# A two-layer backbone in one core: a new order of loads, parts and sums, and token low parts made on GpSimd

## The reference

```python
mod = jnp.split(silu_c @ w_ada[layer] + b_ada[layer], 6)      # mod_c for the context, likewise
a = modulate(rms_norm(h, g[0]), mod[0], mod[1])
o = mixer(a)                                                  # even_mixer or odd_mixer
h = h + mod[2] * rms_norm(o, g[1])
f = jnp.square(jax.nn.relu(modulate(rms_norm(h, g[2]), mod[3], mod[4]) @ w_ff1)) @ w_ff2
h = h + mod[5] * rms_norm(f, g[3])
```

## Time and profile before

| | us |
|---|---|
| median of 3 runs | 1658.23 |
| the profiled execution's own time | 1659.68 |
| its span | 1657.9 |
| TensorE busy | 1576.1 (95%) |
| VectorE busy | 1283.9 (77%) |
| ScalarE busy | 846.7 (51%) |
| GpSimd busy | 156.8 (9%) |
| mean granted TensorE clock | 0.984 of full speed |

### The profile page before, as it was taken

How to read it: one execution, slowest core, us unless ns; L and a number is a source line. 1 busy time by engine, 2 the same in 40 slices (tenths; PEclk the granted TensorE clock), 3 DMA queues, 4 the chain that set the end, 5 groups by cost and what they waited for, 6 DMA issues and landing times.

```text
span 1657.9 us, 24945 instructions
## 1 busy us (share of the span) xinstructions
PE 1576.1 (95%) x9392; PEld 1362.2 (82%) x9392; DVE 1283.9 (77%) x2047; ACT 846.7 (51%) x1515; POOL 156.8 (9%) x171
## 2 busy tenths in 40 slices
PE   7999999999999999969999999889999999999997
PEld 4999888778778999967888777878877778888886
DVE  5889787686689788868889677775785778787778
ACT  5433476774374554545444565214664665444442
POOL 1000275331000000000000000002441000000000
PEclk9999999999999999999999999989999999999999
DMA  8533430014224455585853313433122132322221
GB/s 347 188 124 134 130 87 21 21 52 178 102 99 175 184 216 210 185 323 200 296 202 96 127 53 131 152 124 97 56 77 102 53 126 102 106 105 96 104 99 51
DMA packets 55990, 220.95 MB, mean 133 GB/s; under 512 B 6208, under 2 KB 19392, under 8 KB 41024
## 3 DMA queue, kind: packets, MB, share of 16 engines
q1 hardware_dynamic: 55872, 219.37, 37.6%
HBM read 181.33 MB, written 27.26 MB: 126 GB/s over the span
## 4 chain that ended last, share of the span: by engine, by line
PE 47%; DVE 13%; ACT 5%; DMA 5%; issue 4%; SPq 0%; DVEq 0%; ACTq 0%
PE ps L1827 12%; PE ps L1460 8%; PE ps L1462 8%; PE ps L1461 8%; PE ps L1633 2%; PE ps L1803 2%; PE ps L1606 2%; DMA raw<-in_w_ff 2%; DMA mod_raw<-in_w_ada_t 1%; ACT whi L2632 1%; PE ps L1584 1%; DVE ada_junk L3370 1%; DVE wlo L3620 1%; PE ps L1594 1%; DVE hs L3680 1%
## 5 line engine op out<-in xcount | busy, mean ns | idle before, releaser
L1460 PE MATMUL ps<-whi,ahi 128*128 128x256 f32 (+1 forms) x496 | 150.5, 303 | 4.3 <-DVE wlo L2955 2.4
L1461 PE MATMUL ps<-wlo,ahi 128*128 128x256 f32 (+1 forms) x496 | 148.0, 298 | 0.0
L1462 PE MATMUL ps<-whi,alo 128*128 128x256 f32 (+1 forms) x496 | 147.8, 298 | 0.0
L1827 PE MATMUL ps<-whi,tok_hi 128*128 128x512 f32 x336 | 133.0, 396 | 15.6 <-DVE tok_lo L3690 15.3
L1462 PE MATMUL ps<-ahi,wlo 128*128 128x512 f32 (+2 forms) x368 | 139.6, 379 | 0.0
L1460 PE MATMUL ps<-ahi,whi 128*128 128x512 f32 (+1 forms) x336 | 129.6, 386 | 4.0 <-ACT stage L2436 2.5
L1827 PE MATMUL ps<-whi,tok_lo 128*128 128x512 f32 x336 | 131.5, 391 | 0.0
L1827 PE MATMUL ps<-wlo,tok_hi 128*128 128x512 f32 x336 | 131.5, 391 | 0.0
L1461 PE MATMUL ps<-alo,whi 128*128 128x512 f32 (+1 forms) x336 | 128.8, 383 | 0.0
L3370 DVE SCALAR_TENSOR_TENSOR ada_junk<-mod_raw,silu_rows 128x1024 bf16<-128x1024 f32 x80 | 97.6, 1220 | 29.2 <-DMA mod_raw<-in_w_ada_t 27.2
L2666 ACT ACTIVATE whi<-down_land 128x1024 fp32r<-128x1024 f32 x56 | 59.3, 1058 | 107.9 <-PE ps L1827 101.2
(11 more groups left out here) (362 smaller groups left out, 4351.5 us busy)
## 6 DMA issues: line engine op xcount, KB each, us to landing
raw<-in_w_ff SPq DMA_DIRECT2D x48, 1024.0 KB, 4.8
tok_in<-token_rows SPq DMA_DIRECT2D x56, 384.0 KB, 3.0
mod_raw<-in_w_ada_t SPq DMA_DIRECT2D x16, 1024.0 KB, 7.3
down_land<-in_w_ff SPq DMA_DIRECT2D x32, 512.0 KB, 6.1
token_rows<-hs SPq DMA_DIRECT2D x40, 384.0 KB, 3.1
raw<-in_w_ada_t SPq DMA_DIRECT2D x12, 1024.0 KB, 4.8
mod_raw<-in_w_ada_t SPq DMA_DIRECT2D x24, 512.0 KB, 4.5
raw<-in_w_in_odd SPq DMA_DIRECT2D x9, 1024.0 KB, 4.9
```

Of the source, the lines that this page charges most:

```text
L1460: pe.matmul(dst, lhs[0], rhs[0], start=first, stop=False)
L1461: pe.matmul(dst, lhs[0], rhs[1], start=False, stop=False)
L1462: return pe.matmul(dst, lhs[1], rhs[0], start=False, stop=last)
L1827: ins = pe.matmul(dst, x_[m % 4][:, k, a], w_[:, k, :], start=first and not chained and k == 0 and j == 0, stop=last and k == 1 and j == 2 ...
```

## The change

It reorders work on four engines and moves one kind of it to another.

1. *Output projection of layer 0:* 12 and 4 modulation steps around the low part of unit 2 instead of 8 and 8; the third and fourth pair of modulation rows are loaded one weight unit later.
2. *First phase, column block 1:* the add of c11 comes before the token halves t3, t4 and p7's low part, and two modulation steps move to the block's end.
3. *Start of the second phase:* the b21 blocks of the four quarters are loaded last; stores and modulation units lie between token loads of the first parts; t1, t3, t2 and s4 are summed some parts later; ScalarE and VectorE make part 1's and part 0's weight parts earlier.
4. *GpSimd:* the low part of the token block of part 4 and all later ones, the gate columns of the six tiles and the normalisation of latent tile 2.
5. *End of the layer:* VectorE's roots and residuals go around that; it normalises tile 3 alone.
6. *Input projection:* the rotations of units 0 and 1 come before the modulation steps; the steps are spread 3, 3, 4, 1, 4 and 9 instead of 4, 4, 4, 3, 3, 3, 3; a third buffer takes halves of modulation rows.

The core of the diff:

```diff
-        mod_raw += [place(f"mod_raw{5 + i}", [P, D], F32, C + (24 + 4 * i) * KB) for i in range(2)]
+        mod_raw += [place(f"mod_raw{5 + i}", [P, D], F32, where) for i, where in enumerate((C + 24 * KB, C + 28 * KB, B + 8 * KB))]
...
-                    if r == R_OUT0 + 2:
+                    if r == R_OUT0 + 3:
...
-                        weight_block(0, "b21")
...
-                        weight_block(1, "b11")
-                        weight_block(0, "b12")
-                        weight_block(0, "b22")
+                for name in ("b12", "b22"):
+                    weight_block(0, name)
+                for name in ("b11", "b12", "b22"):
+                    weight_block(1, name)
                 store(7, "a22")
...
+                for name in ("b11", "b12", "b22"):
+                    weight_block(2, name)
                 token_part(2)
                 token_part(3)
...
-                for name in ("s3", "s1", "s2", "a12", "s4"):
-                    store(7, name)
-                modulation_unit(MOD_UP)
-                modulation_unit(MOD_UP + 1)
+                for name in ("b11", "b12", "b22"):
+                    weight_block(3, name)
+                for c in range(4):
+                    weight_block(c, "b21")
                 for m, (name, c) in enumerate(DOWN_PARTS):
                     if m + 4 < len(DOWN_PARTS):
                         token_part(m + 4)
...
+                    if m == 1:
+                        for block_ in ("s3", "s1", "s2", "a12"):
+                            store(7, block_)
+                    elif m in (3, 5):
+                        modulation_unit(MOD_UP + (m - 3) // 2)
+                    elif m == 6:
+                        store(7, "s4")
...
-                    for _ in range(2 if u == 5 else 5):
+                    for _ in range({3: 3, 6: 3, 7: 4, 8: 14}.get(u, 0)):
                         modulation_half(k)
...
                 down_hi(0)
+                down_hi(1)
                 tokens_hi(0)
...
+            def gate_columns(t, part, n=512):
+
+                c0 = 512 * part
+                pool.wait_ge(s_sq, sq_index["post01", t, part] + 1)
+                pool.tensor_tensor(xn[:, t, c0:c0 + n], xn[:, t, c0:c0 + n], gate01[:, 0 if t < NTL else 1, c0:c0 + n],
+                                   ALU.mult).then_inc(s_gated, 1)
...
+            for m in range(TOKENS_BY_POOL, len(DOWN_PARTS)):
+                pool.wait_ge(s_dthi, m + 1)
+                pool.wait_ge(s_dtlo, m)
+                pool.tensor_tensor(tok_lo[m % 4][:, :, :], tok_in[m % 4][:, :, :], tok_hi[m % 4][:, :, :].bitcast(F32),
+                                   ALU.subtract).then_inc(s_dtlo, 1)
+                if m == 52:
+                    wait_groups_before(pool, tg_index["gate01", 0, 1] + 1)
+                    for t in range(NTL):
+                        gate_columns(t, 1)
+            for t in range(NTL):
+                gate_columns(t, 0)
+                if t == 3:
+                    pool.wait_ge(s_rstd, NORM_READY["pre10"] + 1)
+                    pool.tensor_scalar(xn[:, 2, :], h[:, 2, :], norm_rstd[:, 10:11], 1.0, ALU.mult, ALU.mult).then_inc(s_xn, 1)
...
-                    if layer == 1 and u >= 2:
-                        for _ in range(4 if u < 5 else 3):
+                    if layer == 1 and u in (1, 2):
+                        process_odd(u - 1)
+                    if layer == 1:
+                        for _ in range({2: 3, 3: 3, 4: 4, 5: 1, 6: 4}.get(u, 0)):
                             modulation_step()
...
+                    if (layer, u) == (1, 6):
+                        for _ in range(9):
+                            modulation_step()
...
-                    for _ in range(8):
+                    for _ in range(12):
                         modulation_step()
                 split_lo(w0 + 2)
                 if layer == 0:
-                    for _ in range(8):
+                    for _ in range(4):
                         modulation_step()
...
-                    if c == 1:
-                        halves_lo("t3")
-                        halves_lo("t4")
-                    part_lo("p7", c)
+                    if c > 1:
+                        part_lo("p7", c)
...
                     add_block(c, "c11")
+                    if c == 1:
+                        halves_lo("t3")
+                        part_lo("p7", c)
                     part_lo("p3", c)
-                    modulation_step()
+                    if c == 1:
+                        halves_lo("t4")
+                    else:
+                        modulation_step()
...
                     down_lo(m)
-                    tokens_lo(m)
-                    if m == 2:
+                    if m < TOKENS_BY_POOL:
+                        tokens_lo(m)
+                    if m == 4:
                         token_sum_of(7, "s4")
...
-                    if name == "p1":
-                        down_sum_of("t1", c)
-                    elif name == "p3":
-                        down_sum_of("t3", c)
-                        down_sum_of("t2", c)
-                    elif name == ("p2" if c < 4 else "p5"):
+                    if m % 28 in range(2, 6):
+                        down_sum_of("t1", 4 * (m // 28) + m % 28 - 2)
+                    if m % 28 in range(5, 9):
+                        down_sum_of("t3", 4 * (m // 28) + m % 28 - 5)
+                        down_sum_of("t2", 4 * (m // 28) + m % 28 - 5)
+                    if name == ("p2" if c < 4 else "p5"):
                         down_sum_of("t4", c)
...
+                for t in range(3):
+                    settled(t)
+                    residual(post, t)
```

More of the change, by code:

```diff
@@ L560, in build @@
                 sq_list += [(post, t, 1) for t in range(nt)] + [(post, t, 0) for t in range(3)]
-                sq_list += [(pre, 0), (post, 3, 0), (pre, 1), (pre, 2), (pre, 3), (post, 4, 0), (post, 5, 0)]
+                sq_list += [(post, 3, 0)] + [(pre, i) for i in range(4)] + [(post, 4, 0), (post, 5, 0)]
             elif post[5] == "0":
@@ L686, in mod_slot, with half_slot, mod_value @@
                 return 2
-            return 3 + (j - MOD_UP) % 2 if j < MOD_DOWN else 5 + mt
-        def mod_value(j):
+            return 3 + (j - MOD_UP) % 2 if j < MOD_DOWN else half_slot(2 * (j - MOD_DOWN) + mt)
+        slot_of_half = [5 + k % 3 for k in range(15)] + [5 + (k - 15) % 2 for k in range(15, 24)]
+        def half_slot(k):
+            return slot_of_half[k]
+        def mod_value(j, mt):
             if j < 4:
@@ L1042, in straight @@
                         for j in range(2):
[L1043 to L1044 removed]
+                            modulation_pair(j)
                         sp.wait_ge(s_s, S_TOTAL)
@@ L2438, in input_projection @@
                         g += 1
+                    if (layer, u) == (1, 1):
+                        normalize("pre10", 3, (4, 5))
                     if (layer, u) == (1, 2):
@@ L2928, in _ @@
                     zero_rows(1)
+            for m in range(TOKENS_BY_POOL, len(DOWN_PARTS)):
[12 more added lines that the diff above has]
+                    pool.tensor_scalar(xn[:, 2, :], h[:, 2, :], norm_rstd[:, 10:11], 1.0, ALU.mult, ALU.mult).then_inc(s_xn, 1)
+            wait_groups_before(pool, tg_index["gate01", 1, 1] + 1)
+            for t in (4, 5):
+                gate_columns(t, 0, D)
             for i in range(N_ODD):
@@ L3402, in input_projection @@
                             copy_group((f"in{layer}", turned) + fs)
-                    if layer == 1 and u in (1, 2, 4):
-                        process_odd({1: 0, 2: 1, 4: 4}[u])
+                    if (layer, u) == (1, 4):
+                        process_odd(4)
+                    if (layer, u) == (1, 6):
+                        for _ in range(9):
+                            modulation_step()
                     if layer == 0 and groups_of[u]:
@@ L3784, in ff_in_phases @@
                     if m == 55:
[L3785 to L3786 removed]
+                        add_sum(12, "c11", "q20", 0)
+                        add_sum(12, "c11", "q21", 1)
                     down_lo(m)
[L3788 to L3789 removed]
+                    if m < TOKENS_BY_POOL:
+                        tokens_lo(m)
+                    if m == 4:
                         token_sum_of(7, "s4")
[L3791 to L3796 removed]
+                    if m % 28 in range(2, 6):
[4 more added lines that the diff above has]
+                    if name == ("p2" if c < 4 else "p5"):
                         down_sum_of("t4", c)
```

102 lines of the change are left out of this document (38 added, 64 removed).

## The result

| | before | changed |
|---|---|---|
| median | 1658.74 us (4 runs) | 1633.74 us (4 runs, 1632.40 to 1634.84) |
| ratio to before, 95% interval | | 0.985 (0.9833 to 0.9867) |
| span of the profiled execution | 1657.9 us | 1631.2 us |
| mean granted clock | 0.984 | 0.990 |
| VectorE busy | 1283.9 us | 1298.6 us |

What follows compares the result with a forecast made beforehand. VectorE's order, not its mean load, was taken to set the ends of TensorE's waits. Terms 5.4 + 6.5 + 5 - 2.5 + 12.8 = 27.2 us off 1659.7 gave 1632.5, as a median 1631.0 us (range 1614 to 1648).

Steps and rivals of the forecast that it cites:

- the alternation of GpSimd and VectorE: Second products: two-SBUF-input VectorE operations and GpSimd's never overlap; 7 of 12.05 us lost, 5 left; forecast's chance 0.57.
- in the order of the table: Output projection 5.4, first products 6.5, part 4's start 12.05, to part 52 -7, layer's end -2.5, input projection 12.8, rest 0.
- no contention: Rival, second products and layer's end: VectorE and GpSimd overlap freely; 41 us gained, 1617 us; chance 0.19.
- Full alternation: Rival, second products: every VectorE operation waits, PSUM inputs too; 10.4 us lost there, gain 11, 1647 us; chance 0.14.
- GpSimd is the bound: Rival, second products: GpSimd's fp32r low part costs 2.5 us and alternates fully; 1676 us, decisive from 2.16; chance 0.08.
- The late load: Output projection, layer 0: unit loaded behind modulation rows may bring back a wait up to 1.7 us; 1.4 taken.
- what is late next: First products, second column block: p7's then p3's low parts come late next; 2.5 us allowed at the lower end.
- the alternation in parts 4 to 12: Second products: GpSimd and VectorE need 40 to 42 us where TensorE needs 33; some 7 us lost.
- the sum of 217.5 us for both engines: Second products: VectorE 139 and GpSimd 100 us with some 22 overlapping, against TensorE's 216: nearly balanced.
- A loss of 2.5 us: End of the layer: GpSimd's low parts behind gates, gates alternating with residuals; -2.5 us (-6 to 5).
- Alternation of gates and residuals: End of the layer: part 0's four gate products on GpSimd alternate with VectorE's residuals, 2 us more.
- The new wait at the fifth unit: Input projection: 3.1 us wait for a low part delayed by the longer block of rotations, with 2.2 us of clock.

Runs made afterwards that it cites:

- Experiment 1: Changed kernel with all token low parts back on VectorE, GpSimd keeping the gate columns and one normalisation: 1627.00 us, ratio 0.9827.
- Experiment 6: Changed kernel with 8 and 8 modulation steps in layer 0's output projection and its loads in the order of before: 1642.89 us, ratio 0.9906.
- Experiment 4: Changed kernel with column block 1 of the first products in the order of before: 1635.38 us, ratio 0.9873.
- experiment 5: Changed kernel with the modulation step behind the add of c11 from column block 2 on: 1631.30 us, ratio 0.9838.
- experiment 3: Kernel before with only its token low parts from part 4 on moved to GpSimd: 1664.01 us, ratio 1.0047.
- experiment 2: Changed kernel with VectorE also making token low parts 4 to 19, GpSimd only those from 20 on: 1629.32 us, ratio 0.9842.
- 10: Changed kernel with all token low parts on VectorE and the modulation step behind the add of c11: 1623.85 us, ratio 0.9790.
- experiment 11: Kernel of 10 with the end of the layer as before, gate columns and normalisation off GpSimd: 1626.94 us, ratio 0.9806.
- experiment 0: The changed kernel itself, unaltered, timed once more with the second group: 1634.95 us, ratio 0.986.
- experiment 8: Changed kernel with the input projection of before: two buffers, old loads and spread of steps, rotations behind them: 1649.20 us, ratio 0.9942.
- experiment 7: Changed kernel with unit 1's rotation and normalisation in the input projection behind its three modulation steps: 1634.50 us, ratio 0.9859.
- experiment 9: Changed kernel with two buffers for modulation rows in the input projection and loads spread 2, 1, 3, 4, 1, 13: 1651.36 us, ratio 0.9953.

## Why the prediction was right, and where its steps weren't

**The time** came within 3 us of the forecast because the forecast took the alternation of GpSimd and VectorE for granted and still found the rest larger. That it came so close is in part luck: the terms were off by 1.1, -3.4, -0.4, -2.6, 5.0, 1.2 and -1.4 us in the order of the table, and these cancel. Experiment 1 settles that against *no contention* (1617 us, and weight low parts unchanged at 1.22 us; they were 1.82). *Full alternation* is out in its stronger half, that operations with a PSUM input wait too: they take 1.50 us in both. *GpSimd is the bound* was right in one number, 2.22 us for a low part, above its 2.16, but not in what it means: beside an idle VectorE it takes less. GpSimd, then VectorE, at the first two of them:

```profile
731.62 3.80 POOL L2947 TENSOR_TENSOR tok_lo<-tok_in,tok_hi 128x768 fp32r<-128x768 f32 x2 [342.81 <-ACT tok_hi L2679]
...
735.52 0.96 DVE L3719 TENSOR_TENSOR hs<-hs,s_block 128x768 f32<-128x768 f32 x1 [7.96 <-DMA token_rows<-hs]
```

Two in 3.80 us are 1.90 each, near the 1.82 of the earlier trace rows and not the 2.5 of this rival; the rest of the 2.22 is GpSimd waiting for VectorE, and that was in the alternation already.

**Output projection.** 6.5 us against 5.4. The late load came as forecast. VectorE in the changed kernel:

```profile
416.39 1.23 DVE L3402 SCALAR_TENSOR_TENSOR ada_junk<-mod_raw,silu_rows 128x1024 bf16<-128x1024 f32 x1 [2.80 <-DMA mod_raw<-in_w_ada_t]
...
421.56 2.29 DVE L2987 TENSOR_TENSOR wlo<-raw,whi 128x2048 fp32r<-128x2048 f32 x1
...
428.92 2.49 DVE L2998 TENSOR_TENSOR wlo<-raw,whi 128x512 fp32r<-128x512 f32 x4
```

A wait of 2.80 us makes the low part 1.5 us later than in the earlier trace rows, where 1.4 was taken. The step that failed is what this was subtracted from: the quarters had 5.2 us to give and the stall was 3.89, so 5.2 - 1.5 = 3.7 us come off the stall, not 3.89 - 1.4. The quarters begin at 428.92, 3.83 us earlier, and TensorE has no wait left. Experiment 6 gives the price of the two together, 6.1 us by the same products.

**First products.** 3.1 us against 6.5. The stall of the earlier trace rows and its clock went (6.6 us at 534 us), as forecast; "what is late next" was looked for in the low parts of p7 and p3 and was one column block further, the add of c11 of block 2, with the two modulation steps that the change had moved in front of it. Experiment 4 shows the exchange, 2.9 us back for 5.7 bought, and experiment 5 that ahead of this add each step on VectorE costs something in every block.

**Second products.** Part 4 starts 11.6 us sooner where 12.05 was forecast. SyncE's issue of its block, then ScalarE's high part:

```profile
715.86 1.22 SPq L1117 DMA_DIRECT2D tok_in<-token_rows  x2
...
730.69 0.85 ACT L2679 ACTIVATE tok_hi<-tok_in 128x768 fp32r<-128x768 f32 x1 [5.85 <-DMA tok_in<-token_rows]
```

The queue sets the landing, as forecast, and no longer the stores. Its size and its rate were both too small, and the errors cancel: from 706.4 us (716 in the kernel before, less the 9.6 us gained by then) to 730.7 the queue moves at 396 GB/s, 9.6 MB, where 8 MB at 345 GB/s were taken. No run puts the old list of loads back alone, so the 11.6 us rest on the two traces.

Of this, 9.6 are lost until part 52, where 7 were forecast. The runs split them: 5.4 us are the low parts on GpSimd (experiment 1; 6.1 by experiment 3), and 4.2 are left with VectorE making them. All 4.2 lie in parts 4 to 9: TensorE waits twice 1.2 us for low parts that stand behind s4's sum, which VectorE can't begin before 735.6, and behind t1, t2 and t3, and its clock is 0.76 in part 4, some 1.7 us of work. The forecast had put all 7 on the alternation in parts 4 to 12. These parts lose 6.7, so the number was nearly right and its cause wasn't: 2.5 are the alternation. The step that failed is that the rest of the stage was priced at nothing, as the sum of 217.5 us for both engines said that they just fit; the second group's sums and two later places cost 2.9 us (experiment 2). They don't fit evenly: a low part of weights that meets GpSimd's operation takes up to 2.90 us (at 862 us) in a part that has 4.09.

**End of the layer.** A loss of 2.5 us was forecast, a gain of 2.5 measured (-1.4 and 3.9). The 2.5 isn't the sum of what the prediction names (5 us of low parts behind the gates, 2 of alternation, 0.7 back). The latent tiles lost their 1.4 to the first of these, the low parts of parts 53 to 55 behind the four gate products on GpSimd:

```profile
949.43 0.47 PE L1834 MATMUL ps<-whi,tok_hi 128*128 128x512 f32 x1 [1.14 <-POOL tok_lo L2947]
```

Alternation of gates and residuals wasn't it: in experiments 1 and 10 the gates stay on GpSimd, and with the low parts on VectorE nothing is lost there (17.8 us of lead late in part 52 and at the transposes in experiment 1, 20.8 and 20.8 in 10). What was left out is the context tiles: their two gates leave VectorE, its residuals and roots come sooner, and the wait of 2.5 us before the products at 1005 us goes (experiment 11), with the lower clock that followed it in the kernel before, 0.64 over 1005.3 to 1010. The step that failed is that only one of two chains was priced.

**Input projection.** 14.0 us against 12.8 (13.1 in experiment 0's profile), and 14 to 15 by experiment 8. VectorE waits for modulation rows 14.1 us instead of 27.2, in ten waits, where 12.7 in nine were forecast:

```profile
DVE ada_junk L3402 <- DMA mod_raw<-in_w_ada_t: 14.1, 10, 2.3
```

The new wait at the fifth unit is there with 2.23 us instead of 3.1. Of the reasons one fell: putting the rotations ahead of the steps gains nothing (experiment 7). What is left are the spread of steps and loads and the third buffer, together. The new spread of steps with two buffers and that list of loads gains nothing (experiment 9); three buffers with the old spread, and two with a better list, were not run, so how the 14 us divide stays open.

**What isn't explained:** 1.4 us are given back after the third scores, 0.9 of them at 1288 us, where the granted clock is at its lower level in the changed kernel and not in the one before. The change itself doesn't make it so: experiment 0, the same kernel, has a clock of 1.00 behind the same place (1291 to 1297 us), where the first profile has 0.74 (1287.4 to 1294), and in both TensorE has waited 1.66 us just before. It gives back 1.7 us right behind the third scores in its place, with a clock of 0.76 over 1110 to 1117.

## What to carry to other kernels

GpSimd is no second VectorE: work with two SBUF inputs that is moved to it can cost VectorE up to its whole length there when they meet, 1.8 to 2.2 us for 0.95 us saved here. In parts where VectorE had time this cost TensorE nothing, in the busy ones it cost 5.4 us; the gates paid, since they left a chain for which TensorE waits. Work that nobody waits for soon (the modulation steps) belongs behind the operation that the next engine waits for, and moving it out of one such place needs a look at the next one. And look at what stands behind a load in SyncE's list that must wait for a buffer or a stored block: with the stores moved behind part 4's block, part 4 came 11.6 us sooner, and one half of modulation rows without a buffer held a weight unit back by 35 us (experiment 9, which lost 15 to 17).

## What the runs showed of the hardware beyond that

Even small operations stand still beside GpSimd. VectorE, then GpSimd, in the changed kernel at the end of the second products:

```profile
949.34 1.22 DVE L3015 TENSOR_SCALAR chy<-chv 128x3 int32<-128x3 int32 x1
950.59 1.20 DVE L3022 TENSOR_TENSOR cha<-chy 128x3 f32<-128x3 f32 x1
...
949.25 3.77 POOL L2919 TENSOR_TENSOR xn<-xn,gate 128x512 f32<-128x512 f32 x3
```

Three numbers a partition take 1.22 us instead of 0.17 (the same operation at 961.65), about an operation of GpSimd each (3.77/3 = 1.26), though the first of the two has one tile as its input. The next in this chain takes 1.21, so three of them cost 3.6 us instead of 0.5, as much as three operations of 128x1024.

The clock behind a short wait varies. Of TensorE's waits here those of 2.08 us at 1110 and 2.64 at 551 were not followed by a lower clock, those of 2.16 at 713, 2.53 at 740 and 2.23 at 1020 were: the granted clock of 714 to 718 is 0.57, of 740 to 746 0.72, of 1021 to 1025 0.57, and of 552 to 558 and 1111 to 1117 1.00. In the earlier trace rows a wait of 2.61 us stayed without one too. And one and the same wait, 2.52 us ahead of the products behind the context tiles, was followed by 0.64 in the kernel before (1005.3 to 1010) and by 1.00 in experiment 11 (986.97 to 991.5). So whether a wait of 2 to 3 us is paid twice can't be read from its length, which is where two of the prediction's terms had their bounds.
